# Two attention stages of a two-block transformer kernel: the order of a few steps inside their slots

## What is computed

```
c = jnp.cumsum(log_f, axis=1)
s = jnp.einsum('bqhd,bkhd->bhqk', qi, k) * scale
s = s + ci[..., None] - c_keys
s = jnp.where(k_pos[None, :] <= q_pos[:, None], s, -jnp.inf)
p = jax.nn.softmax(s, axis=-1)
out = jnp.einsum('bhqk,bkhd->bqhd', p, v)
```

```
q = rmsnorm((h @ wq).reshape(bsz, seq, X_HEADS, X_HD), gq)
k = rmsnorm((m @ wk).reshape(bsz, n_mem, X_HEADS, X_HD), gk)
v = (m @ wv).reshape(bsz, n_mem, X_HEADS, X_HD)
s = jnp.einsum('bshd,bmhd->bhsm', q, k) * (X_HD ** -0.5)
p = jax.nn.softmax(s, axis=-1)
o = jnp.einsum('bhsm,bmhd->bshd', p, v).reshape(bsz, seq, X_HEADS * X_HD)
return o @ wo
```

## Time and profile before

| | us |
|---|---|
| median of 3 runs | 2975.14 |
| lowest and highest of them | 2971.48, 2977.38 |
| profiled execution, its time | 2983.45 |
| its span, first to last instruction | 2981.7 |
| PE busy | 2927.8 (98%) |
| DVE, ACT, POOL busy | 1120.7, 1091.1, 1282.0 |
| mean granted TensorE clock | 0.993 |

### The profile page before, as it was taken

The page is one execution under the profiler, slowest core; times in us unless marked ns, Lnnn a source line. Parts: engine busy times, 40 slices in busy tenths (PEclk is TensorE's granted clock), DMA queues, the critical chain, the costliest instruction groups (busy, mean ns, idle before and its releaser), DMA issues.

```text
span 2981.7 us, 36176 instructions
## 1 busy us (share of the span) xinstructions
PE 2927.8 (98%) x13036; PEld 2334.5 (78%) x13036; DVE 1120.7 (38%) x1664; ACT 1091.1 (37%) x1504; POOL 1282.0 (43%) x588
## 2 busy tenths in 40 slices
PE   8999999999999999999999999999999999999999
PEld 6888877888888888887888886665688888788887
DVE  4223156322313221135322216489588363332210
ACT  4232265332323222244332333466344444332321
POOL 4444444444444444443444443157532372244443
PEclk9999999999999999999999999999999999999999
DMA  4333322333333333332333331111222342133332
GB/s 150 98 97 98 94 85 76 94 98 98 90 93 99 98 93 88 100 104 81 99 98 105 90 108 52 50 50 60 82 75 61 92 148 70 51 99 97 93 93 77
DMA packets 80653, 267.50 MB, mean 90 GB/s; under 512 B 11168, under 2 KB 13216, under 8 KB 80560
## 3 DMA queue, kind: packets, MB, share of 16 engines
q1 hardware_dynamic: 77904, 262.01, 29.3%
q10 hardware_dynamic: 2656, 4.26, 0.5%
HBM read 263.09 MB, written 2.10 MB: 89 GB/s over the span
## 4 chain that ended last, share of the span: by engine, by line
PE 91%; DVE 4%; issue 2%; ACT 2%; POOL 1%; ACTq 0%; DVEq 0%; POOLq 0%
PE bank L429 27%; PE bank L430 27%; PE bank L431 27%; PE bank L475 1%; PE bank L476 1%; PE bank L477 1%; PE bank L2351 1%; PE bank L1084 1%; PE bank L2071 1%; PE bank L2091 0%; POOL w_lo L417 0%; PE bank L1497 0%; DVE s_g L1625 0%; PE bank L1506 0%; PE bank L689 0%
## 5 line engine op out<-in xcount | busy, mean ns | idle before, releaser
L417 POOL TENSOR_TENSOR w_lo<-w_stage,w_hi 128x1024 fp32r<-128x1024 f32 (+1 forms) x448 | 1057.5, 2363 | 1463.6 <-ACT w_hi L393 1463.5
L429 PE MATMUL bank<-xg_hi,w_hi 128*128 128x512 f32 x2400 | 953.1, 397 | 16.1 <-DVE xg_lo L2689 10.9
L430 PE MATMUL bank<-xg_lo,w_hi 128*128 128x512 f32 x2400 | 938.8, 391 | 0.0
L431 PE MATMUL bank<-xg_hi,w_lo 128*128 128x512 f32 x2400 | 937.9, 391 | 0.0
L393 ACT ACTIVATE w_hi<-w_stage 128x1024 fp32r<-128x1024 f32 (+2 forms) x500 | 514.9, 1033 | 550.1 <-PE bank L431 506.0
L429 PEld LDWEIGHTS bank<-xg_hi,w_hi 128*128 128x128 f32 x2400 | 453.2, 189 | 142.0 <-issue 45.1
L430 PEld LDWEIGHTS bank<-xg_lo,w_hi 128*128 128x128 f32 x2400 | 453.6, 189 | 96.0 <-issue 3.8
L431 PEld LDWEIGHTS bank<-xg_hi,w_lo 128*128 128x128 f32 x2400 | 453.2, 189 | 95.8
L431 PE MATMUL bank<-h_hi,w_lo 128*128 128x512 f32 x880 | 346.7, 394 | 0.0
L429 PE MATMUL bank<-h_hi,w_hi 128*128 128x512 f32 x880 | 346.7, 394 | 0.0
L430 PE MATMUL bank<-h_lo,w_hi 128*128 128x512 f32 x880 | 346.7, 394 | 0.0
(11 more groups left out here) (461 smaller groups left out, 2971.3 us busy)
## 6 DMA issues: line engine op xcount, KB each, us to landing
w_stage<-w_up SPq DMA_DIRECT2D x220, 512.0 KB, 3.5
w_stage<-w_down SPq DMA_DIRECT2D x80, 512.0 KB, 3.5
w_stage<-merge SPq DMA_DIRECT2D x36, 512.0 KB, 3.6
w_stage<-w_down SPq DMA_DIRECT2D x40, 384.0 KB, 3.1
w_stage<-hg_qfg SPq DMA_DIRECT2D x12, 512.0 KB, 3.6
w_stage<-rec_r SPq DMA_DIRECT2D x8, 512.0 KB, 3.5
w_stage<-rec_y SPq DMA_DIRECT2D x8, 512.0 KB, 3.7
w_stage<-rec_out SPq DMA_DIRECT2D x8, 512.0 KB, 3.5
```

Source lines behind the costliest of these rows:

```text
L417: pool.tensor_tensor(w_lo[:, r, 0:w], w_stage[:, r, 0:w], f32(w_hi[:, r, 0:w]), ALU.subtract).then_inc(w_lo_ready, 1)
L429: pe.matmul(out, w_hi[:, r, c], hi, start=start, stop=False)
L430: pe.matmul(out, w_hi[:, r, c], lo, start=False, stop=False)
L431: return pe.matmul(out, w_lo[:, r, c], hi, start=False, stop=stop)
```

## The change

Six moves of steps inside their slots; no instruction is added or taken away.

- PE, cross attention: in slots 6, 10 and 14 `transposes(n - 2)` stands ahead of the head outputs (slot 18 has no transposes). In slot 17 `xo_part` still comes ahead of the transposes.
- ACT, cross attention: the squares of the query tiles stand ahead of `copies(n - 2)`.
- DVE, cross attention: `q_tile` stands ahead of `scale(n - 1)`.
- ACT, forgetful attention: `high` stands between `exps(j, 0)` and `copies(j - 1, 1)` instead of at the end of iterations 5, 9 and 13.
- DVE, forgetful attention: `dve_fox_low` stands between `scale(j, 0)` and `scale(j, 1)` instead of at the end of those iterations.

```diff
@@ dve_mix
-            for o in range(2):
-                scale(j, o)
+            scale(j, 0)
+            if j >= 5 and j % 4 == 1:
+                dve_fox_low(dve, j // 4 - 1)
+            scale(j, 1)
             if j - 1 in UNIT_AT:
...
-            if j >= 5 and j % 4 == 1:
-                dve_fox_low(dve, j // 4 - 1)
@@ act_mix
             if j >= 1:
                 copies(j - 1, 0)
             exps(j, 0)
+            if j >= 5 and j % 4 == 1:
+                high(j // 4 - 1)
             if j >= 1:
                 copies(j - 1, 1)
...
-            if j >= 5 and j % 4 == 1:
-                high(j // 4 - 1)
@@ pe_cross
                 scores(n)
-            if cross_head_out(n) is not None:
-                outputs(cross_head_out(n))
             if n == X_STEPS + 1:
                 xo_part(*XO_PART_AT[n])
             if 0 <= n - 2 < X_STEPS:
                 transposes(n - 2)
+            if cross_head_out(n) is not None:
+                outputs(cross_head_out(n))
@@ dve_cross
+            if n - 1 in Q_HALF_AT and Q_HALF_AT[n - 1][1]:
+                q_tile(Q_HALF_AT[n - 1][0])
             if 0 <= n - 1 < X_STEPS:
                 scale(n - 1)
-            if n - 1 in Q_HALF_AT and Q_HALF_AT[n - 1][1]:
-                q_tile(Q_HALF_AT[n - 1][0])
@@ act_cross
+            for u in X_SQUARES_AT.get(n, ()):
+                act_head_square(act, "q", u)
             if 0 <= n - 2 < X_STEPS:
                 copies(n - 2)
-            for u in X_SQUARES_AT.get(n, ()):
-                act_head_square(act, "q", u)
```

## The result

| | before | after |
|---|---|---|
| median | 2977.28 us (16 runs) | 2964.28 us (16 runs) |
| lowest, highest | 2971.38, 2986.71 | 2960.80, 2973.54 |
| ratio, 95% interval | | 0.9958, 0.9948 to 0.9967 |
| span of the profiled execution | 2981.7 | 2971.7 |
| its mean granted clock | 0.993 | 0.993 |

Between the medians the change gains 13.0 us; the ratio, 0.42%, makes it 12.5. The forecast was 12 us and 2963. In the course of the study the kernel before was timed again with each group of kernels; its medians were 2977.3, 2978.2, 2980.4 and 2977.4 us.

What follows compares the result with a forecast made beforehand. PE, busy 98% of the span, was taken to bound the kernel, so only its waits count. Direct gains of 6 us plus half the clock part, 6 us, took 2975.1 to 2963 us, range 2957 to 2971.

Steps and rivals of the forecast that it cites:

- only PE's waits count: Whole kernel: PE is busy 98% of the span, so another engine counts only where PE waits for it.
- slot 6: Cross attention: the squares are ready under the head outputs, PE's wait goes, direct gain 1.67 us.
- slot 11: Cross attention: the stall ahead of the sums falls to 0.30 us, direct gain 0.86 us.
- slot 16: Cross attention, slots 14 to 17: PE still waits about 0.90 us for the scale, direct gain 1.26 us.
- the sum: Both stages, profiled execution: direct 3.79 + 2.2 us, clock 8.57 + 3.16 us, together 17.7 us.
- The next wait: Forgetful attention, slots 6, 10, 14: second transposes wait for ACT's copy for o = 0; direct sum 2.2 of 3.4 us.
- rival D: Forgetful attention: moved parts delay other steps, `spreads` waits for the query norm on PE; slower, 2983 us at worst, chance 0.05.
- half of them: Both stages: half of the clock part, 6 us, counted towards the median, from the spread of three timed runs.
- rival B: Both stages: stalls only, few falls in timed runs or remaining 0.3 and 0.9 us stalls cause them; 2969 to 2971, chance 0.17.
- signs of being wrong: Profile after: clock at 0.50 behind slot 11 or 16, or new PE waits over 1 us for `probT` copies, `kf` and `qn`.
- A: Both stages, the forecast itself: stalls and most clock falls go, 2957.4 to 2969 us, chance 0.70.
- C: Both stages: a new wait for each old one, direct gain under 2 us, clock as before, 2973 to 2976, chance 0.08.

Runs made afterwards that it cites:

- changed_again: The changed kernel timed and profiled once more, with nothing altered against it: 2966.6 us, ratio 0.9958 to before.
- fill: The kernel before, plus 18 useless matmuls on PE in the stalls of cross attention slots 6, 11 and 16: 2973.3 us, ratio 0.9985.
- fox_only: Against the kernel before, only the moves in forgetful attention, cross attention left as before: 2972.8 us, ratio 0.9980.

## Why the prediction was right

**Bound and direct gains.** The reading "only PE's waits count" held, and the steps were sized well: slot 6 1.67 us expected, all of it gone; slot 11 0.86 expected, 0.85 measured (sums 1.61 us into the slot, 2.46 before); slot 16 a wait of 0.90 expected, 0.73 measured, so 1.43 us instead of 1.26. The stage without a fall (changed_again) takes 78.04 us against 82.11 in fill, which keeps the old stalls: 4.07 us direct, where the sum had 3.79.

**Forgetful attention.** Expected 0.6, 0.8 and 0.8 us for slots 6, 10 and 14. Measured against fill, whose slot 6 took 11.27 us without a fall (1872.78 to 1884.05): 11.27 - 10.47 = 0.80, then 10.65 - 9.85 = 0.80 and 9.31 - 8.63 = 0.68, in all 2.28 us for 2.2. The next wait was the one named, ACT's first copy, by 0.82, 0.20 and 0.20 us. The `spreads` matmul did not come to wait for the query norm, on which rival D hung.

**Clock.** The sizes were right: 8.0 us for the three falls of cross attention (8.57 in the sum) and 14.44 - 11.27 = 3.17 us for slot 6 of forgetful attention (3.16). That half of them would count in the median was a guess from the spread of three runs, so it is partly luck that the forecast of 12 us lies within 1 us of the measured gain; the pair of profiled executions gave 10.0 us where the sum had 17.7. The runs' own mean clocks bear it out roughly: 0.9943 over 31 runs of before and 0.9968 over 16 of after, and over the runs of all kernels timed up to then 0.001 of mean clock went with 2.4 us, which makes 6 us of the 13 clock and 7 direct. The 2.4 is a fit within kernels; for single kernels it comes out between 2.0 and 3.3, which makes the clock part 5 to 8 us.

**What was wrong.** That all falls go in cross attention: behind slot 11 a stall of 0.30 us was still followed by one in three of five profiled executions, for 1.6 us. That is a part of rival B, at one of the two places it named. The prediction argued from stalls of about 0.9 us without a fall, those in slots 10 and 14 of forgetful attention. The same trace holds the opposite: in slot 2 a stall of 0.86 us was followed by a fall of 1.6 us, so forgetful attention held more falls than the one counted (slot 0 held one as well, also 1.6 us). In slot 11 sums of single columns follow the stall, which may be why so short a one was enough; no run separates that from the stall. This is also one of the prediction's own signs of being wrong: a clock of 0.50 behind slot 11 although the stall is shorter. And the mean clock of the profiled execution did not rise to 0.995: falls in unchanged stages came in their place; over the 16 runs it did rise. The take ahead of the scale was costed at nothing, which is right, and it also brings nothing.

**Rivals.** A held. B's stalls-only is out by `fill`, which gained with every stall in its old place. C is out: each wait that came in place of an old one was shorter by the worked amounts. D is out by `fox_only`, 6.0 us faster.

The page of the Trainium skill that the prediction cites for run-variable falls (TensorE: Matmul & The Clock Gate, Part 1: The HAM clock gate) agrees with these runs: the same kernel had a fall behind slot 11 in one profiled execution and none in the next, and its timed runs lie between clocks of 0.993 and 0.998.

## What to carry to other kernels

Where TensorE is 98% busy, list its own waits by line and ask of each what stands ahead of the late step on its engine: here a copy that waited for TensorE stood ahead of a square that did not. A stall of one or two microseconds can cost as much again in clock (in before 1.6 to 3.4 us at each of six places, though nothing behind the 1.20 us in slots 4 and 8 of forgetful attention), so work that needs nothing new (half the head outputs, a piece of a projection) belongs exactly there; if there is none, idle matmuls still paid 4.5 us here. Take the gain of such a change from many runs, since a single pair of traces carried 6 us of falls in stages that had not changed.

## What the runs showed of the hardware

- 18 matmuls whose results nobody reads, put into 5.0 us of idle time (about 4.1 us of work by 0.23 us each, an estimate from the spacing of such matmuls here), made the kernel 4.5 us faster. The granted clock over cross attention is 1.00 in the profile of fill and 0.92 in that of before.
- A stall of 0.30 us followed by 16 single-column instructions was followed by a fall to the lower level in three of five executions; the same sums with no stall ahead had none in any profile, in slots 2, 6 or 11.
- A stall of 1.20 us in slots 4 and 8 of forgetful attention was followed by no fall in ten profiles, one of 0.86 us in slot 2 came with a fall in eight of ten.
- Within one kernel the time rises as the mean granted clock falls, by 2 to 3 us for 0.001: after had 2960.8 us at 0.998 and 2973.5 at 0.993.
